# One-hot gate rows of a routed expert layer: which engine compares, which engine scales

## The chip, the cores and the metric

The kernel runs as one program on one core of one Trainium2 chip. Its time is the device time of that core in microseconds (us), from one launch to its end. Engines are named as in the profile: PE is TensorE, DVE is VectorE, ACT is ScalarE, SP issues the weight transfers.

## What is computed

The reference is a two-layer transformer block, followed by a second block of two layers whose feed-forward part is a product-key expert layer (`peer_ffn`). The change touches that last part alone, which runs twice, once for each layer:

```
idx = i1 * PEER_N_KEYS + i2            # 256 tokens x 128 choices (8 heads x 16)
g = jax.nn.softmax(best, axis=-1)
act = gelu(einsum('ckd,cd->ck', u_tab[ic], xc))
out = einsum('ck,ckd->cd', gc * act, v_tab[ic])
```

There are 128 x 128 experts, each named by a first key i1 and a second key i2. The kernel doesn't gather experts. It computes the scores of all experts and multiplies them by a dense gate matrix which is zero where a token did not choose the expert. For one token that matrix is a product of two one-hot matrices: with the token's 128 choices c as the contraction, gate[k2, k1] = sum over c of first[c, k1] * second[c, k2], where first[c, k1] is 1 where i1 of choice c is k1, and second[c, k2] is g[c] where i2 of choice c is k2, else 0.

## The kernel before

Stages follow one another: modulation, an even and an odd mixer with their feed-forward parts, then for each of two layers a mixer (class `Mixer`) and the expert layer (class `Peer`). Each engine has its own instruction list, written out in program order, and the lists meet at semaphores. Nothing is reordered at run time: an instruction that waits holds up all that stand behind it on its engine.

In `Peer`, after the queries and the early scores (`EarlyScores`: the scores of the first 33 of 128 slices of the experts), `Route` picks the experts on DVE and leaves, for all 256 tokens, the tile `slots` [128 choices, 3, 256 tokens]: gate, first key, second key. Then comes `Gates`, and after it `Experts`, which streams the u and v tables and does most of the layer's matrix work. `Experts` begins when `Gates` is done.

`Gates` takes the tokens in 64 groups of four. For each group g:

- DVE `make(g)`: one comparison of the row 0..127 (`iota`) with four tokens' second keys gives `second` [128, 4 x 128] (L1957; the tile lies in a part of `hT` that is free here, so the trace calls it hT), signal `second_made`; one with the first keys gives `first` (L1959), signal `first_made`. From g = 4 on it waits first until PE has read the buffers four groups back.
- ACT `scale(g)` waits for `second_made` and multiplies the second rows by the gates, token by token, in place: four ACTIVATEs of 128 x 128 (L1979), signal `scaled`.
- PE waits for `first_made`, for `scaled` and for its bank, and does four products of 128 x 128 x 128 into one of four PSUM banks (L1938). In the trace each product of f32 operands shows as two MATMULs, so that a group has eight.
- ACT `move_late(g)` waits for the bank and copies columns 33 to 127 of the four tokens into `gates` (L1986, 128 x 380 elements), signal `moved`.
- DVE `weigh_early(g)` waits for `moved` and multiplies the first 33 columns of the bank by the early scores (L1965, 128 x 132 elements), which frees the bank.

The order on DVE is make(g), weigh_early(g - 2), make(g + 1), and so on; on ACT it is move_late(g - 2), scale(g), move_late(g - 1), and so on. Behind the last group ACT loads the table of Gelu (`warm`, L149) and `Experts` starts with L2119 on ACT.

Of the kernel before, what the change touches and what calls it, by code (L numbers as in the profile page):

```python
# [10 lines left out]
ACT = mybir.ActivationFunctionType  # L11
ALU = mybir.AluOpType
AX = mybir.AxisListType

P = 128
# [33 lines left out]
class Span:  # L49


    def __init__(self, sem, first):
        self.sem, self.first = sem, first
# [17 lines left out]
class Use:  # L71
# [3 lines left out]
    def __init__(self, tensor, written, read):  # L75
        self.tensor, self.written, self.read = tensor, written, read
# [11 lines left out]
class Bank:  # L88
    def __init__(self, tensor, written, read):
        self.tensor, self.written, self.read = tensor, written, read  # L90
# [69 lines left out]
def hold(engine, marks):  # L160

    for sem, count in marks:
        engine.wait_ge(sem, count)
# [81 lines left out]
class Fetch:  # L245
# [7 lines left out]
    def scalar(self, after=()):  # L253
        hold(self.nc.scalar, after)
        for dst, src in self.pairs:
            self.nc.scalar.dma_start(dst, src).then_inc(self.landed.sem, 16)
# [14 lines left out]
class Modulation:  # L271
# [24 lines left out]
    def tensor(self):  # L296
        k, pe = self.k, self.k.nc.tensor
        pe.wait_ge(*self.split.after(2))
        hold(pe, self.fetch.done)
        for _ in range(4):  # L300
            pe.matmul(k.bank[7].tensor[:, 0:2], k.ones[:], k.ones[:, 0:2], start=True, stop=True)
        for b in range(self.BLOCKS + 1):
            if b == self.BLOCKS:
                self.turn(b - 1)
                break
            use = self.rows[b]
            pe.wait_ge(*use.free())
            for c in range(DC):
                hi, lo = k.ring.take()
                pe.matmul(use.tensor[0:4, :], self.parts[:, c, :], hi, start=(c == 0), stop=False)  # L310
                last = k.ring.free(pe.matmul(use.tensor[0:4, :], self.parts[:, c, :], lo, start=False,
                                             stop=(c == DC - 1)))
                if b > 0 and c == 2:
                    self.turn(b - 1)
# [497 lines left out]
class Attention:  # L812
# [6 lines left out]
    def __init__(self, k, groups, keys, span, scale, prob, turned, after):  # L819
        self.k, self.groups, self.keys, self.span, self.scale = k, groups, keys, span, scale  # L820
        self.prob, self.turned, self.after = prob, turned, after
        self.scores = [[k.bank[r].use() for r in range(4)] for _ in range(groups)]
        self.turns = [[k.bank[4 + st % 2].use() for st in range(span)] for _ in range(groups)]
        self.max = k.named("row_max").take(4 * groups)
        self.neg = k.named("row_max_negated").take(2 * groups)
        self.sunk = k.named("sink_weighed").take(2 * groups if self.sink is not None else 0)
        self.den = k.named("row_sum_inverted").take(groups)
        self.by_scalar = k.named("weights_by_scalar").take(2 * groups)
        self.by_vector = k.named("weights_by_vector").take(2 * groups)
        self.mx, self.negm, self.sums, self.rec, self.extra = (k.stats[:, :, 4 * j:4 * j + 4] for j in range(5))  # L830
# [1080 lines left out]
class Gates:  # L1911
# [5 lines left out]
    def __init__(self, k, slots, iota, early, gates, first, second, routed):  # L1917
        self.routed = routed
        self.k, self.slots, self.iota, self.early, self.gates = k, slots, iota, early, gates
        self.first, self.second = first, second  # L1920
        self.uses = [k.bank[g % 4].use() for g in range(self.GROUPS)]
        self.second_made = k.named("second_key_rows").take(self.GROUPS)
        self.first_made = k.named("first_key_rows").take(self.GROUPS)
        self.scaled = k.named("rows_scaled").take(self.GROUPS)
        self.moved = k.named("gates_moved").take(self.GROUPS)
        self.done = [u.emptied() for u in self.uses[-4:]] + [self.moved.after(self.GROUPS)]

# [3 lines left out]
    def tensor(self):  # L1931
        pe = self.k.nc.tensor
        for g, use in enumerate(self.uses):
            pe.wait_ge(*self.first_made.after(g + 1))
            pe.wait_ge(*self.scaled.after(g + 1))
            pe.wait_ge(*use.free())
            for t in range(4):
                m = pe.matmul(use.tensor[:, t * P:(t + 1) * P], self.first[:, g % 4, t, :], self.rows(g, t),  # L1938
                              start=True, stop=True)
            m.then_inc(use.written.sem, 1)  # L1940
# [7 lines left out]
                self.weigh_early(g - 2)  # L1948

    def make(self, g):  # L1950
        dve = self.k.nc.vector
        row_no = self.iota[:].unsqueeze(1).to_broadcast([P, 4, P])
        tokens = slice(4 * g, 4 * g + 4)
        keys = [self.slots[:, j, tokens].unsqueeze(2).to_broadcast([P, 4, P]) for j in (1, 2)]
        if g >= 4:
            dve.wait_ge(*self.uses[g - 4].full())
        dve.tensor_tensor(self.second[g % 4], row_no.rearrange("p (c k) n -> p c k n", c=2),  # L1957
                          keys[1].rearrange("p (c k) n -> p c k n", c=2), ALU.is_equal).then_inc(self.second_made.sem, 1)
        dve.tensor_tensor(self.first[:, g % 4], row_no, keys[0], ALU.is_equal).then_inc(self.first_made.sem, 1)  # L1959

    def weigh_early(self, g):
        dve, use = self.k.nc.vector, self.uses[g]
# [3 lines left out]
                          ALU.mult).then_inc(use.read.sem, 1)  # L1966

    def scalar(self):
        for g in range(self.GROUPS + 2):
            if g >= 2:  # L1970
                self.move_late(g - 2)
            if g < self.GROUPS:
                self.scale(g)

    def scale(self, g):
        act = self.k.nc.scalar
        act.wait_ge(*self.second_made.after(g + 1))
        for t in range(4):
            m = act.activation(self.rows(g, t), self.rows(g, t), ACT.Copy,  # L1979
                               scale=self.slots[:, 0, 4 * g + t:4 * g + t + 1])  # L1980
        m.then_inc(self.scaled.sem, 1)

    def move_late(self, g):
        act, use = self.k.nc.scalar, self.uses[g]
# [460 lines left out]
```

## Time and profile before

| | |
|---|---|
| median of 3 runs | 3836.66 us |
| fastest run | 3831.36 us |
| slowest run | 11778.27 us |
| the profiled execution: its own time | 3843.8 us |
| its span, first to last instruction | 3842.5 us |
| mean granted clock of PE over the span | 0.923 |
| PE busy | 3449.5 us (90%) |
| DVE busy | 2288.9 us (60%) |
| ACT busy | 1810.7 us (47%) |

The shares of busy time are means over all stages. What the change can do is read in the two windows in which `Gates` runs, 1868.8 to 1984.1 us (first layer) and 3081 to 3196 us (second layer) from the start of the span. The slowest run stands far from the other two; the median is one of these two.

### The profile page before, as it was taken

The page shows a single profiled execution, that of the slowest core. Times are in us where ns is not written, and L with a number is a line of the kernel's source. Part 1 is how long each engine was busy: PE and PEld are TensorE (multiplying, and loading weights), DVE is VectorE, ACT ScalarE, POOL GpSimd, SP SyncE. Part 2 cuts the span into 40 slices and gives each one's busy share as a digit, 9 for nine tenths or more (in the row PEclk, how much of TensorE's full clock was granted, in tenths as well). Part 3 has the DMA queues.
Part 4 walks back from the last instruction along what each step waited for, and adds up shares of the span by engine and source line. Part 5 has one row for each costly group of instructions (what it writes and reads, how often), then busy time and mean ns, then how long its engine had stood idle before and what let it go on. Part 6 is the DMA issues. An engine that isn't in the chain of part 4 may idle for free.

```text
span 3842.5 us, 51118 instructions
## 1 busy us (share of the span) xinstructions
PE 3449.5 (90%) x19132; PEld 2853.0 (74%) x19132; DVE 2288.9 (60%) x4729; ACT 1810.7 (47%) x3796; POOL 0.2 (0%) x4
## 2 busy tenths in 40 slices
PE   7899889999979989589779999998869968999999
PEld 2474447887748988388668999997659857899998
DVE  6633334333465645768876666665665986666665
ACT  6622333332344534252585555554334196555554
POOL 0000000000000000000000000000000000000000
PEclk9897888999889989589999999998769999999999
DMA  8820001223203543044115555553204403555554
GB/s 310 286 99 11 1 23 66 99 90 94 94 5 110 179 139 122 0 138 143 66 53 184 186 187 187 186 186 128 72 26 161 160 1 125 186 186 186 186 186 154
DMA packets 134925, 479.90 MB, mean 125 GB/s; under 512 B 15384, under 2 KB 17304, under 8 KB 133912
## 3 DMA queue, kind: packets, MB, share of 16 engines
q1 hardware_dynamic: 130352, 463.53, 36.1%
q10 hardware_dynamic: 4328, 13.11, 0.9%
q8 instruction: 154, 2.52, 0.3%
q14 instruction: 91, 0.75, 0.1%
HBM read 475.53 MB, written 1.05 MB: 124 GB/s over the span
## 4 chain that ended last, share of the span: by engine, by line
PE 83%; DVE 9%; issue 3%; DMA 3%; ACT 3%; ACTq 0%; DVEq 0%
PE bank L608 14%; PE bank L610 13%; PE bank L609 13%; PE bank L2089 6%; PE bank L2088 6%; PE bank L2090 6%; PE bank L2014 6%; PE bank L1938 4%; PE bank L475 3%; PE bank L882 3%; DMA raw<-in_mod_w 2%; DVE conv L1313 1%; PE bank L484 1%; PE bank L892 1%; PE bank L1119 1%
## 5 line engine op out<-in xcount | busy, mean ns | idle before, releaser
L223 DVE TENSOR_TENSOR w_lo<-raw,w_hi 128x512 fp32r<-128x512 f32 x1664 | 1124.5, 691 | 798.3 <-ACT w_hi L214 769.0
L214 ACT ACTIVATE w_hi<-raw 128x512 fp32r<-128x512 f32 x1664 | 1011.9, 626 | 814.3 <-PE bank L610 606.6
L608 PE MATMUL bank<-x_hi,w_hi 128*128 128x256 f32 x2096 | 597.5, 285 | 14.9 <-DVE w_lo L223 7.3
L609 PE MATMUL bank<-x_lo,w_hi 128*128 128x256 f32 x2096 | 595.5, 284 | 0.0
L610 PE MATMUL bank<-x_hi,w_lo 128*128 128x256 f32 x2096 | 593.4, 283 | 0.0
L608 PEld LDWEIGHTS bank<-x_hi,w_hi 128*128 128x128 f32 x2096 | 398.1, 190 | 26.4 <-issue 8.2
L2088 PE MATMUL bank<-w_hi,wt_hi 128*128 128x512 f32 x1024 | 406.2, 397 | 6.5 <-DVE wt_lo L2146 6.5
L2089 PE MATMUL bank<-w_lo,wt_hi 128*128 128x512 f32 x1024 | 407.5, 398 | 0.0
L2090 PE MATMUL bank<-w_hi,wt_lo 128*128 128x512 f32 x1024 | 405.8, 396 | 0.0
L609 PEld LDWEIGHTS bank<-x_lo,w_hi 128*128 128x128 f32 x2096 | 398.2, 190 | 8.0
L610 PEld LDWEIGHTS bank<-x_hi,w_lo 128*128 128x128 f32 x2096 | 399.9, 191 | 0.0
L608 PE MATMUL bank<-a_hi,w_hi 128*128 128x512 f32 (+1 forms) x880 | 309.1, 351 | 18.0 <-DVE a_lo L580 18.0
L610 PE MATMUL bank<-a_hi,w_lo 128*128 128x512 f32 (+1 forms) x880 | 303.9, 345 | 0.0
L609 PE MATMUL bank<-a_lo,w_hi 128*128 128x512 f32 (+1 forms) x880 | 302.0, 343 | 0.0
L2014 PE MATMUL bank<-xn,u_raw 128*128 128x256 f32 x1056 | 228.2, 379 | 0.0
L2088 PEld LDWEIGHTS bank<-w_hi,wt_hi 128*128 128x128 f32 x1024 | 193.5, 189 | 45.9 <-DVE wt_lo L2146 6.9
L2090 PEld LDWEIGHTS bank<-w_hi,wt_lo 128*128 128x128 f32 x1024 | 193.2, 189 | 46.2
L1938 PE MATMUL bank<-hT,first 128*128 128x128 f32 x1024 | 147.5, 289 | 83.1 <-issue 77.2
L2089 PEld LDWEIGHTS bank<-w_lo,wt_hi 128*128 128x128 f32 x1024 | 193.8, 189 | 38.0
L2014 PEld LDWEIGHTS bank<-xn,u_raw 128*128 128x128 f32 x1056 | 200.5, 190 | 27.2
L1938 PEld LDWEIGHTS bank<-hT,first 128*128 128x128 f32 x1024 | 127.0, 195 | 103.7 <-issue 97.4
L608 PEld LDWEIGHTS bank<-a_hi,w_hi 128*128 128x128 f32 x880 | 167.6, 190 | 47.3 <-issue 13.9
(318 smaller groups left out, 4947.5 us busy)
## 6 DMA issues: line engine op xcount, KB each, us to landing
raw<-in_v SPq DMA_DIRECT2D x256, 512.0 KB, 4.4
raw<-in_u SPq DMA_DIRECT2D x190, 512.0 KB, 3.5
raw<-in_mod_w SPq DMA_DIRECT2D x96, 512.0 KB, 4.8
raw<-in_w_gate_up SPq DMA_DIRECT2D x88, 512.0 KB, 3.5
u_raw<-in_u SPq DMA_DIRECT2D x66, 512.0 KB, 3.5
raw<-in_w_in SPq DMA_DIRECT2D x40, 512.0 KB, 4.0
raw<-in_w_down SPq DMA_DIRECT2D x32, 512.0 KB, 3.5
raw<-in_w_peer SPq DMA_DIRECT2D x32, 512.0 KB, 3.9
```

Of the source, the lines that this page charges most:

```text
L214: self.nc.scalar.activation(self.hi[:, m % 4, :], self.half(m), ACT.Copy).then_inc(self.rounded[m % 4], 1)
L223: self.nc.vector.tensor_tensor(self.lo[:, m % 4, :], self.half(m), self.hi[:, m % 4, :], ALU.subtract).then_inc(self.ready[m % 4], 1)
L475: m = pe.matmul(self.sums.tensor[:, 4 * at:4 * at + P // group], k.sq[:, n % 4, t * P:(t + 1) * P], indicators[group], start=(n == 0 and t ...
L608: pe.matmul(out[:, 0:width], hi[:, w], x_hi, start=(c == 0), stop=False)
L609: pe.matmul(out[:, 0:width], hi[:, w], x_lo, start=False, stop=False)
L610: mm = pe.matmul(out[:, 0:width], lo[:, w], x_hi, start=False, stop=(c == total - 1))
L882: m = pe.matmul(use.tensor[:, 0:self.keys[r]], l, x, start=(j == 0), stop=(j == len(pairs) - 1))
L1938: m = pe.matmul(use.tensor[:, t * P:(t + 1) * P], self.first[:, g % 4, t, :], self.rows(g, t), start=True, stop=True)
L2014: m = pe.matmul(use.tensor[:, 0:LAT], self.raw[:, t % 3, c * P:(c + 1) * P], self.xn[:, c, :], start=(c == 0), stop=(c == DC - 1))
L2088: pe.matmul(out, self.wt_hi[:, s, rows], hi, start=(t == 0), stop=False, skip_group_check=True)
L2089: pe.matmul(out, self.wt_hi[:, s, rows], lo, start=False, stop=False, skip_group_check=True)
L2090: m = pe.matmul(out, self.wt_lo[:, s, rows], hi, start=False, stop=(t == NKEY - 1), skip_group_check=True)
```

## The change

On DVE the comparison of the second keys and the multiplication by the gate become one `tensor_scalar` for each token, with two operands of one value per partition (second key and gate): four instructions of 128 x 128 in place of one of 128 x 512. The comparison of the first keys stays one instruction, but of three tokens (128 x 384). ACT no longer scales. It makes the first-key row of the fourth token instead, in two dependent steps: Abs(key - iota), then Relu(1 - that), which is 1 where the key is met and 0 elsewhere. Its wait for `second_made` goes; it waits once for the route's result and, from g = 4 on, for the buffers. PE waits for `first_made`, `second_made` and `last_made`.

```
-        self.scaled = k.named("rows_scaled").take(self.GROUPS)
+        self.last_made = k.named("first_key_last_row").take(self.GROUPS)
...
             pe.wait_ge(*self.first_made.after(g + 1))
-            pe.wait_ge(*self.scaled.after(g + 1))
+            pe.wait_ge(*self.second_made.after(g + 1))
+            pe.wait_ge(*self.last_made.after(g + 1))
...
     def make(self, g):
-        dve = self.k.nc.vector
-        row_no = self.iota[:].unsqueeze(1).to_broadcast([P, 4, P])
-        tokens = slice(4 * g, 4 * g + 4)
-        keys = [self.slots[:, j, tokens].unsqueeze(2).to_broadcast([P, 4, P]) for j in (1, 2)]
+
+        dve, n = self.k.nc.vector, 4 * g
         if g >= 4:
             dve.wait_ge(*self.uses[g - 4].full())
-        dve.tensor_tensor(self.second[g % 4], row_no.rearrange("p (c k) n -> p c k n", c=2),
-                          keys[1].rearrange("p (c k) n -> p c k n", c=2), ALU.is_equal).then_inc(self.second_made.sem, 1)
-        dve.tensor_tensor(self.first[:, g % 4], row_no, keys[0], ALU.is_equal).then_inc(self.first_made.sem, 1)
+        for t in range(4):
+            m = dve.tensor_scalar(self.rows(g, t), self.iota[:], self.slots[:, 2, n + t:n + t + 1],
+                                  self.slots[:, 0, n + t:n + t + 1], ALU.is_equal, ALU.mult)
+        m.then_inc(self.second_made.sem, 1)
+        dve.tensor_tensor(self.first[:, g % 4, 0:3], self.iota[:].unsqueeze(1).to_broadcast([P, 3, P]),
+                          self.slots[:, 1, n:n + 3].unsqueeze(2).to_broadcast([P, 3, P]),
+                          ALU.is_equal).then_inc(self.first_made.sem, 1)
...
     def scalar(self):
+        hold(self.k.nc.scalar, self.routed)
         for g in range(self.GROUPS + 2):
             if g >= 2:
                 self.move_late(g - 2)
             if g < self.GROUPS:
-                self.scale(g)
-
-    def scale(self, g):
-        act = self.k.nc.scalar
-        act.wait_ge(*self.second_made.after(g + 1))
-        for t in range(4):
-            m = act.activation(self.rows(g, t), self.rows(g, t), ACT.Copy,
-                               scale=self.slots[:, 0, 4 * g + t:4 * g + t + 1])
-        m.then_inc(self.scaled.sem, 1)
+                self.last_row(g)
+
+    def last_row(self, g):
+
+        k, act, row = self.k, self.k.nc.scalar, self.first[:, g % 4, 3]
+        if g >= 4:
+            act.wait_ge(*self.uses[g - 4].full())
+        away = k.sstep(act.activation(row, self.iota[:], ACT.Abs, bias=self.slots[:, 1, 4 * g + 3:4 * g + 4],
+                                      scale=-1.0))
+        act.wait_ge(*away)
+        act.activation(row, row, ACT.Relu, bias=self.k.ones[:, 0:1], scale=-1.0).then_inc(self.last_made.sem, 1)
```

## Rows read from the trace of the kernel before

**Rows 1.** Busy time of each engine in the two windows of `Gates` (x: instructions).
```profile
core 0: us, PE busy (x) PEld busy (x) DVE busy (x) ACT busy (x) POOL busy (x), PEclk, DMA share, GB/s
1869.00:1987.00 118.00, 74.24 (x514) 63.92 (x515) 105.13 (x195) 115.67 (x325) 0.00 (x0) 0.98 0.00 1
3081.00:3200.00 119.00, 75.36 (x517) 64.80 (x518) 105.46 (x195) 115.65 (x325) 0.00 (x0) 0.97 0.00 1
```

**Rows 2.** Who waited for whom in 1869 to 1987 us: total, times, longest.
```profile
PE bank L1938 <- issue: 38.6, 62, 0.6
```

**Rows 3.** Instructions in order of time, 1918 to 1922 us: start, length, engine, line.
```profile
1918.48 0.97 ACT L1986 ACTIVATE gates<-bank 128x380 f32<-128x380 f32 x1
...
1918.84 1.13 PE L1938 MATMUL bank<-hT,first 128*128 128x128 f32 x8 [0.63 <-issue]
1919.10 1.39 ACT L1979 ACTIVATE hT<-hT,slots 128x128 f32<-128x128 f32 x4
1919.49 0.43 DVE L1965 TENSOR_TENSOR early<-bank,early 128x132 f32<-128x132 f32 x1
1919.83 0.68 DVE L1957 TENSOR_TENSOR hT<-iota,slots 128x512 f32<-128x512 f32 x1
1920.24 0.97 ACT L1986 ACTIVATE gates<-bank 128x380 f32<-128x380 f32 x1
...
1920.59 1.13 PE L1938 MATMUL bank<-hT,first 128*128 128x128 f32 x8 [0.62 <-issue]
```

**Rows 4.** In order of time, the stage's first groups, 1868 to 1875 us.
```profile
1868.79 0.69 DVE L1957 TENSOR_TENSOR hT<-iota,slots 128x512 f32<-128x512 f32 x1
1869.39 0.68 DVE L1959 TENSOR_TENSOR first<-iota,slots 128x512 f32<-128x512 f32 x1
1869.51 2.48 ACT L1979 ACTIVATE hT<-hT,slots 128x128 f32<-128x128 f32 x8 [3.76 <-DVE hT L1957]
...
1870.89 3.75 PE L1938 MATMUL bank<-hT,first 128*128 128x128 f32 x16 [2.94 <-DVE first L1959]
```

**Rows 5.** In order of time, the stage's last group, 1982 to 1984 us.
```profile
1982.13 1.13 PE L1938 MATMUL bank<-hT,first 128*128 128x128 f32 x8 [0.63 <-issue]
...
1983.30 0.80 ACT L1986 ACTIVATE gates<-bank 128x380 f32<-128x380 f32 x1 [0.56 <-PE bank L1938]
```

**Rows 6.** Groups of DVE instructions over the whole span, shapes kept apart: busy, mean ns.
```profile
L970 DVE TENSOR_SCALAR prob<-prob,stats 128x512 f32<-128x512 f32 x32 | 14.7, 482 | 0.3
L458 DVE COPY spread<-mean_col 128x512 f32<-128x512 f32 x15 | 6.4, 427 | 0.5
L1872 DVE TENSOR_SCALAR part_i<-best_i 128x128 uint32<-128x128 uint32 x8 | 1.8, 223 | 0.1
L1310 DVE TENSOR_SCALAR conv<-pad,gvec 128x256 f32<-128x256 f32 x4 | 1.2, 350 | 0.1
L1869 DVE TENSOR_TENSOR res<-best 128x128 f32<-128x128 f32 x4 | 1.2, 292 | 0.1
```

**Rows 7.** DVE in order of time: two TENSOR_SCALAR in a row, at two places.
```profile
1565.78 0.62 DVE L1310 TENSOR_SCALAR conv<-pad,gvec 128x256 f32<-128x256 f32 x2
...
348.19 0.75 DVE L970 TENSOR_SCALAR prob<-prob,stats 128x256 f32<-128x256 f32 x2
```

**Rows 8.** Groups of ACT instructions over the whole span: with a value per partition, and without.
```profile
L561 ACT ACTIVATE a_hi<-a_scaled,modT 128x256 fp32r<-128x256 f32 x56 | 27.6, 506 | 24.7 <-DVE a_scaled L573 24.7
L517 ACT ACTIVATE x_hi<-xn 128x256 fp32r<-128x256 f32 x16 | 6.6, 417 | 7.8 <-DVE xn L528 7.8
```

**Rows 9.** L1979 alone in 1868 to 1878 us: least, median and greatest length.
```profile
L1979 ACT ACTIVATE hT<-hT,slots x20: 355/387/403, 1869.5 to 1877.9; 128x128 f32<-128x128 f32 x20
```

**Rows 10.** ACT in order of time: a load of a function table, and two dependent steps.
```profile
8.25 1.28 ACT L336 ACT_TABLE_LOAD   x1
9.54 0.22 ACT L336 ACTIVATE silu_c<-cT 128x16 f32<-128x16 f32 x1
9.79 0.22 ACT L338 ACTIVATE parts<-silu_c 128x16 fp32r<-128x16 f32 x1
```

## The prediction

> **What bounds the kernel now.** Read first the busy time in the two windows of `Gates`: ACT is busy for 115.67 of 118 us, DVE for 105.13, PE for 74.24, and no data moves [rows 1]. Both layers look alike, so one is worked out and doubled. Then the waits: PE has 62 short waits of 0.6 us, one for almost every group, put down to "issue" [rows 2]. The order of time says what they are [rows 3]. ACT's four scalings run from 1919.10 to 1920.49 and PE's next group starts at 1920.59, so PE starts each time 0.10 us behind the last scaling. DVE's L1965 starts at 1919.49, just behind the end of the copy L1986 (1918.48 + 0.97 = 1919.45), and so DVE too is kept by ACT. ACT itself never stops: copy to copy is 1.76 us (1918.48 to 1920.24), of which copy to first scaling is 0.62 and the four scalings 1.14, or 0.285 each. ACT bounds the stage, at 1.755 us per group, the mean over many groups (between the PE starts 1918.84 and 1920.59 it is 1.75).
>
> The stage lasts from the first comparison, 1868.79, to the end of the last copy, 1984.10: 115.3 us [rows 4, 5]. Twice that is 6% of the span, which is the ceiling of what can happen here in either direction unless the stage becomes much longer. Behind it everything is released by it: `Experts` starts when ACT has done the last copy and the table load, so each microsecond of the stage is one of the kernel. What ran before is finished and no transfer is due in it, so nothing outside covers a gain or a loss.
>
> **What ACT does after.** It loses four scalings, 1.14 us, and gets two dependent steps. Neither function is in this trace; their cost is that of ACTIVATEs of the size with a value per partition. L1979 is such a one, 355 to 403 ns long [rows 9], and 128x256 with a bias per partition is 506 against 417 ns without [rows 8], so the kind of value hardly matters. The wait between the steps costs the overlap: two dependent steps stand 0.25 apart at a length of 0.22, a gap of 0.03 [rows 10]. So: copy to Abs 0.62, Abs to Relu 0.39 + 0.03 = 0.42, Relu to the next copy 0.285, sum 1.32 us per group. The other bound is the ring through PE: move_late(g) stands before last_row(g + 2), and PE(g) between last_row(g) and move_late(g). From rows 3 to 5: 0.10 to start PE, 1.13 of PE, 0.04 to start the copy, 0.62 + 0.42 + 0.39 until the Relu's end, in all 2.70 us for two groups, 1.35 for one. ACT and this ring therefore allow 1.32 to 1.35 and are left 0.4 below the time of now. The new hold for the route is met when DVE begins; ACT sits idle there anyhow (3.76 us) [rows 4].
>
> **What DVE does after.** This decides. Now it needs, when nothing holds it, 0.60 for each comparison of 128x512 (1868.79 to 1869.39) [rows 4] and 0.34 for L1965 (1919.49 to 1919.83) [rows 3]: 1.54 per group. After:
> - The comparison of three tokens: TENSOR_TENSORs of 128x512 and of 128x128 last 0.685 us [rows 4] and 0.292 us (L1869) [rows 6], so a column costs 1.02 ns. 128 columns fewer make 0.60 - 0.13 = 0.47.
> - Four TENSOR_SCALARs of 128x128. Columns: with one value per partition 128x512 takes 482 ns and 128x256 350 ns [rows 6], so 256 columns cost 132 ns, half of what a TENSOR_TENSOR takes for them, and 128 cost 66. Fixed: two of 128x256 in a row cover 0.62 at 0.35 each, so they start 0.27 apart [rows 7]; less 0.13 for columns that leaves nearly 0.14, and 0.20 for each of 128x128, if the second value per partition costs nothing more.
> - The price of a value per partition: 482 ns against 427 for a COPY of the same size with none (L458) [rows 6], 55 ns. No row has two. The second is worth between 0 (fetched beside the first) and 55 ns (fetched after it), so 0.20 to 0.255 each, four of them 0.79 to 1.02.
> - An upper bound for the fixed part: the two L970 of 128x256 start 0.75 - 0.35 = 0.40 apart [rows 7]. If that is the rule for the kind of instruction, it leaves up to 0.27 fixed and 0.33 each. They work in place, which the new ones don't; L1310 reads one tile and writes another as the new ones do, so it is the nearest row.
> - L1965 is unchanged, 0.34 to 0.35.
>
> With the second value free: 0.79 + 0.47 + 0.35 = 1.61 us per group. With it at full price: 1.02 + 0.47 + 0.35 = 1.84. Both lie over ACT's 1.35: DVE takes ACT's place as the bound, and the question is on which side of 1.755 it comes out. There is no row that tells the two apart. I take the first: the 55 ns are a latency rather than a quantity (one value in each partition), and latencies of two reads of one instruction need not add up. That is an argument and no measurement, so both ends stay in the range.
>
> A rule speaks against my fixed part. The Trainium skill, "VectorE: DVE Perf Modes", section on the TRN2 errata, gives VectorE SBUF to SBUF 58 cycles and the columns over the mode's factor, 120 from PSUM. By it the new list would be 4 x 0.127 + 0.46 + 0.26 = 1.23 us, less than ACT's bound (an estimate from that page). The page itself says that this row comes out too short for one instruction alone. The trace's 0.14 fixed for one with a value per partition is more than double its 0.06, and L1965's 0.34 is over its 0.26.
>
> **PE.** It has one wait more. Its group takes 1.13 [rows 3], under 1.61, so it isn't the bound. Its start is now released by DVE's last comparison instead of ACT's scalings. The granted clock in the window is 0.98 now [rows 1]; a busier PE gives no ground for a lower one, and I take it as it is.
>
> **The sum.** DVE's list from the first TENSOR_SCALAR to the end of the last comparison: 64 x (0.79 + 0.47) = 80.6 and 62 x 0.35 = 21.7, 102.3 us. Behind it 0.08 for the end of that comparison, 0.10, PE 1.13, 0.04 and the copy 0.80 [rows 5]: 2.15. At the start PE's first two groups go at half pace (3.75 for 16 MATMULs against 1.13 for 8) [rows 4] and make DVE's first waits for a copy come late by about 0.5. Stage: 105.0 us against 115.3, 10.3 less, twice 20.6. The profiled execution would go from 3843.8 (span 3842.5 and 1.3 around it) to 3823.2. It lies 7.1 over the median of the runs; from 3836.66 the forecast is 3816 us, 0.54% less.
>
> **The rivals.**
> - Second value at full price (slower than before). The list is 64 x (1.02 + 0.47) + 21.7 + 2.15 = 119.2 us, 3.9 more than now, twice 7.8: 3844 us. DVE is the place, the fetch of the gate the price; it decides from 0.235 us per TENSOR_SCALAR on, where 4 x 0.235 + 0.82 meets 1.755. For it: one value costs a visible 55 ns. Against it: nothing but the argument above.
> - A dearer TENSOR_SCALAR: a spacing of 0.33 as the in-place pairs show, or a fused comparison that is given only a TENSOR_TENSOR's pace, one column per 1.02 ns. At 0.33, 4 x 0.13 = 0.52 more per group, 67 us over the forecast: 3883. At the slow pace, 4 x 0.065 x 128 = 33 more: 3849, or 3877 with the second value dear as well. Against it: L1872, an integer shift of 128x128, takes 223 ns [rows 6], 69 less than the TENSOR_TENSOR of 128x128, so it has the quick pace.
> - Cheap DVE, ACT's ring the bound: 64 x 1.35 + 3 = 89 us per stage, 26 less, twice 52: 3784. It needs TENSOR_SCALARs 0.13 apart, and no row is so quick. The errata row of the page named above would give this.
> - Abs and Relu not in the loaded table. Each load takes 1.28 [rows 10]; with two per group ACT would need 1.32 + 2.57 = 3.89, the stage 252 us, the kernel 4110. Against it: Copy, Square and Identity run between Exp, Sqrt and Gelu here with no load of their own. The Trainium skill, "ScalarE: Activation LUTs", section on table sets, says that relu, copy, identity and abs are in every set; no run here shows it of Abs and Relu.
> - The change does nothing that can be seen: DVE's spacing happens to be 0.22 to 0.24, the stage stays at 1.7 to 1.76 and ACT's relief is idle time. This is the middle of the first two cases: 3825 to 3837.
>
> **How the numbers follow.** Forecast case (second value free or nearly) 0.45; at full price 0.33; the middle 0.07; dearer TENSOR_SCALAR 0.08; cheap DVE 0.05; table loads 0.02. The forecast's own range is 3808 to 3824, from 0.19 to 0.21 per TENSOR_SCALAR and the edges of the stage. The range over cases has to hold forecast, middle and full price (0.85), whose ends with some microseconds of spread between runs (the two close ones are 5 us apart) are 3806 and 3856. A change within 2% (77 us, about what a measurement of this kernel can tell from no change) covers all but table loads and a very dear TENSOR_SCALAR: 0.03 slower, 0.01 faster.
>
> **What would show it.** In the changed profile: DVE busy without gaps through the stage and ACT with an idle time of some 0.3 us per group; the group's period (from one L1965 to the next) 1.61 if right, 1.84 if the second value costs; the TENSOR_SCALAR's length 0.28 against 0.34; its starts 0.20 or 0.255 apart; PE's gaps of 0.6 shrunk to 0.48 and ended by DVE; the Abs to Relu distance 0.42; one ACT_TABLE_LOAD at the stage's end and none inside. What would make me wrong beyond the cases: a wait of DVE at L1965 for the copy in each group, which would mean that the ring through PE is longer than the 1.35 worked out.

## The result and the profile after

The changed kernel takes 3843.09 us (median of 15 runs) against 3835.70 us (the kernel before, 15 runs too); ratio 1.0016, 95% interval 1.0009 to 1.0023. It is slower by some 6 us, which is little, but the interval excludes 1. Ratios here and below compare fast runs alone, without one run of 11778.27 us of the kernel before and one of 8801.40 us of the kernel with three rows scaled and one fused. The forecast was 3816 us; the rival with the second value at full price had 3844. Which of the two it is stands in the stage itself.

Busy time of each engine in the two windows of the stage, changed kernel (answers to [rows 1]):

```profile
core 0: us, PE busy (x) PEld busy (x) DVE busy (x) ACT busy (x) POOL busy (x), PEclk, DMA share, GB/s
1869.00:1987.00 118.00, 75.37 (x498) 62.60 (x496) 111.25 (x363) 87.00 (x188) 0.00 (x0) 0.97 0.02 5
3081.00:3200.00 119.00, 76.00 (x508) 63.35 (x508) 113.92 (x373) 89.34 (x194) 0.00 (x0) 0.97 0.01 4
```

In this execution the stage begins and ends some microseconds earlier than in the one of before, so that the windows also hold some 8 us of `Experts` in the first layer. The exchange is plain all the same: ACT falls from 115.67 to 87.00 us, DVE rises from 105.13 to 111.25. A window that lies inside the first layer's stage in both executions shows it clean, first before, then after (columns as above):

```profile
1880.00:1960.00 80.00, 51.55 (x366) 44.31 (x367) 74.12 (x138) 80.00 (x230) 0.00 (x0) 1.00 0.00 1
```
```profile
1880.00:1960.00 80.00, 50.96 (x352) 42.59 (x352) 80.00 (x264) 60.82 (x132) 0.00 (x0) 1.00 0.00 1
```

Before, ACT was the engine that never stopped; after, DVE is. The waits of the first layer's stage (answers to [rows 2]) name the new bound:

```profile
PE bank L1939 <- DVE first L1960: 39.4, 60, 0.7
ACT gates L1992 <- PE bank L1939: 24.3, 59, 1.0
DVE early L1968 <- ACT gates L1992: 1.4, 1, 1.4
```

PE waits in each group for DVE's last comparison, ACT waits in each group for PE, and DVE waits once, for the last copy, when all its comparisons are done. One group in order of time (answers to [rows 3]):

```profile
1918.62 0.41 DVE L1968 TENSOR_TENSOR early<-bank,early 128x132 f32<-128x132 f32 x1
...
1918.75 0.36 ACT L1984 ACTIVATE first<-iota,slots 128x128 f32<-128x128 f32 x1
1918.75 1.16 PE L1939 MATMUL bank<-hT,first 128*128 128x128 f32 x8 [0.66 <-DVE first L1960]
1918.95 1.10 DVE L1957 TENSOR_SCALAR hT<-iota,slots 128x128 f32<-128x128 f32 x4
1919.14 0.40 ACT L1987 ACTIVATE first<-first,ones 128x128 f32<-128x128 f32 x1
1919.95 0.82 ACT L1992 ACTIVATE gates<-bank 128x380 f32<-128x380 f32 x1 [0.40 <-PE bank L1939]
1919.97 0.54 DVE L1960 TENSOR_TENSOR first<-iota,slots 128x384 f32<-128x384 f32 x1
1920.44 0.41 DVE L1968 TENSOR_TENSOR early<-bank,early 128x132 f32<-128x132 f32 x1
```

Read the starts on DVE, not the lengths: product to first TENSOR_SCALAR 0.33, four TENSOR_SCALARs 1.02, comparison to product 0.47, in all 1.82 us from product to product. 1.02 for four is 0.255 each. Over the whole run:

```profile
L1957 DVE TENSOR_SCALAR hT<-iota,slots x512: 327/331/468, 1861.1 to 3191.5; 128x128 f32<-128x128 f32 x171
L1984 ACT ACTIVATE first<-iota,slots x128: 357/366/401, 1861.1 to 3190.6; 128x128 f32<-128x128 f32 x128
L1960 DVE TENSOR_TENSOR first<-iota,slots x128: 537/541/676, 1862.2 to 3191.7; 128x384 f32<-128x384 f32 x128
```

A TENSOR_SCALAR with two values per partition lasts 0.331 us, where 0.28 had been expected with one price and 0.34 with two. The stage's edges, first steps and table load of each layer:

```profile
1861.13 1.11 DVE L1957 TENSOR_SCALAR hT<-iota,slots 128x128 f32<-128x128 f32 x4
...
1979.08 1.28 ACT L149 ACT_TABLE_LOAD   x1
...
3194.48 1.28 ACT L149 ACT_TABLE_LOAD   x1
```

From first step to table load the stage takes 117.95 us, and 115.3 before ([rows 4, 5]; the last copy's end is 1984.10). The second layer's stage, 3076.54 to 3194.48, takes 117.9, and 115.3 before. That is 2.6 us more in each, 5.3 in all, inside the interval of the ratio (3 to 9 us). There is no load of a table inside the stage. Nothing outside it is needed to explain the result. The two profiled executions as wholes can't show it: they took 3843.8 us before and 3843.66 after, because the rest of the kernel differs by as much from run to run as the stages do by the change.

### The profile page after: what moved, and what is told of

Same layout as the page of the kernel before. It is cut to its first block, busy times and chain, and to the rows that moved or that the text cites. A ratio compares the mean times of both kernels' runs of the same rounds, so it can differ in the third digit from the quotient of the medians.

```text
span 3842.3 us, 51376 instructions
## 1 busy us (share of the span) xinstructions
PE 3446.5 (90%) x19132; PEld 2850.7 (74%) x19132; DVE 2314.0 (60%) x5113; ACT 1762.4 (46%) x3540; POOL 0.2 (0%) x4
## 4 chain that ended last, share of the span: by engine, by line
PE 78%; DVE 15%; DMA 3%; ACT 3%; issue 1%; ACTq 0%; DVEq 0%
PE bank L608 14%; PE bank L610 13%; PE bank L609 13%; PE bank L2095 6%; PE bank L2094 6%; PE bank L2096 6%; PE bank L2020 6%; DVE hT L1957 3%; PE bank L475 3%; DMA raw<-in_mod_w 3%; PE bank L882 2%; DVE first L1960 2%; DVE conv L1313 1%; DVE early L1968 1%; PE bank L484 1%
```

## The experiments

The nine kernels below were each timed beside runs of the kernel before, four runs for most, ten for "changed without the last row" and "three scaled, one fused", six for "GpSimd fuses one". "Stage" is the first layer's, from DVE's first step to the table load, in the profiled execution; "group" is the spacing of DVE's products or of ACT's copies in the steady part.

| kernel | group, us | stage, us | ratio to before | 95% interval |
|---|---|---|---|---|
| before | 1.755 | 115.3 | 1 | |
| changed | 1.82 | 117.9 | 1.0016 | 1.0009 to 1.0023 |
| one value, two operations | 1.58 | 103.2 | 0.9942 | 0.9925 to 0.9958 |
| one value, one operation | 1.58 | 103.1 | 0.9938 | 0.9921 to 0.9954 |
| no value, two operations | 1.43 | 94.9 | 0.9898 | 0.9882 to 0.9915 |
| all first rows on DVE | 1.95 | 127.0 | 1.0060 | 1.0044 to 1.0077 |
| changed without the last row | 1.82 | 117.9 | 1.0018 | 1.0005 to 1.0030 |
| before with three scalings | 1.53 | 101.0 | 0.9930 | 0.9904 to 0.9957 |
| three scaled, one fused | 1.65 | 107.9 | 0.9972 | 0.9958 to 0.9987 |
| GpSimd scales one | 1.54 | 102.3 | 0.9931 | 0.9909 to 0.9953 |
| GpSimd fuses one | 1.46 | 97.6 | 0.9920 | 0.9901 to 0.9939 |

**What makes a TENSOR_SCALAR dear.** Theory 1: the values per partition are fetched one after the other. Theory 2: the second arithmetic operation costs time. Theory 3: this kind of instruction has a floor at 0.257 us. Three kernels differ in the per-token step alone.

```
# changed
m = dve.tensor_scalar(self.rows(g, t), self.iota[:], self.slots[:, 2, n + t:n + t + 1],
                      self.slots[:, 0, n + t:n + t + 1], ALU.is_equal, ALU.mult)
# one_value_two_ops
m = dve.tensor_scalar(self.rows(g, t), self.iota[:], self.slots[:, 2, n + t:n + t + 1], 1.0, ALU.is_equal, ALU.mult)
# one_value_one_op
m = dve.tensor_scalar(self.rows(g, t), self.iota[:], self.slots[:, 2, n + t:n + t + 1], None, ALU.is_equal)
# no_value_two_ops
m = dve.tensor_scalar(self.rows(g, t), self.iota[:], 5.0, 0.01, ALU.is_equal, ALU.mult)
```

> The changed kernel, but the per-token comparison multiplies by the constant 1.0 and not by the token's gate (left out: the gates' weight). Theory 1, values per partition are fetched one after the other at 0.055 us each: the four TENSOR_SCALARs start 0.20 us apart where the changed kernel has 0.257, the group takes 0.80 + 0.79 = 1.59 us against 1.82, and the kernel is 24 us faster than before (ratio 0.994). Theory 2, the second arithmetic operation costs it: still 0.257 apart, 1.82 us per group, 6 us slower than before (ratio 1.0016). Theory 3, nothing starts closer than 0.257 for this kind of instruction: as theory 2.

> The changed kernel, but the per-token step only compares (one value per partition, one operation; left out: the gates' weight). Theory 1: as with two operations, 0.20 us apart, 1.59 us per group, 24 us faster than before (0.994). Theory 2: 0.20 apart here and 0.257 with two operations. Theory 3: 0.257 apart, ratio 1.0016.

> The changed kernel, but the per-token step compares with the constant 5 and multiplies by the constant 0.01 (left out: second keys and gates). Theory 1: no value to fetch, 0.145 us apart, DVE's list 0.58 + 0.79 = 1.37 us per group, just over the 1.35 worked out for the ring through PE and ACT; 50 us faster than before (0.987). If the ring is really longer, the group takes the ring's time and DVE shows a wait for the copy in each group. Theory 2: 0.257 apart and 1.82 us. Theory 3: the same.

The step's instructions over the whole run (least, median and greatest length), in the order of the three kernels:

```profile
L1957 DVE TENSOR_SCALAR hT<-iota,slots x512: 267/280/356, 1863.1 to 3165.2; 128x128 f32<-128x128 f32 x171
```
```profile
L1957 DVE TENSOR_SCALAR hT<-iota,slots x512: 267/279/333, 1860.2 to 3162.1; 128x128 f32<-128x128 f32 x171
```
```profile
L1957 DVE TENSOR_SCALAR hT<-iota x512: 206/220/234, 1864.9 to 3151.2; 128x128 f32<-128x128 f32 x171
```

Median lengths of 0.331, 0.280 and 0.220 us for two values, one and none; the least lengths, 0.327, 0.267 and 0.206, stand 0.06 apart at both steps. One operation or two is the same, 0.279 and 0.280. The starts say it too. Four in a row, in order of time, one kernel after the other (one value and two operations; one value and one; none and two):

```profile
1920.24 0.90 DVE L1957 TENSOR_SCALAR hT<-iota,slots 128x128 f32<-128x128 f32 x4
...
1921.02 0.58 DVE L1960 TENSOR_TENSOR first<-iota,slots 128x384 f32<-128x384 f32 x1
```
```profile
1920.48 0.86 DVE L1957 TENSOR_SCALAR hT<-iota,slots 128x128 f32<-128x128 f32 x4
...
1921.26 0.54 DVE L1960 TENSOR_TENSOR first<-iota,slots 128x384 f32<-128x384 f32 x1
```
```profile
1921.46 0.61 DVE L1957 TENSOR_SCALAR hT<-iota 128x128 f32<-128x128 f32 x4
...
1922.00 0.54 DVE L1959 TENSOR_TENSOR first<-iota,slots 128x384 f32<-128x384 f32 x1
```

First step to the comparison behind it is 1.02 us with two values, 0.78 with one and 0.54 with none: 0.255, 0.195 and 0.135 each, steps of 0.06. Theories 2 and 3 fall, and of theory 1 the price stands: each value adds 0.06, also the second. That the values are fetched one after the other is the picture behind it, which no run shows. The ratios are 0.9942 and 0.9938; theory 1 expected 0.994 for both kernels, theory 2 only for the one with one operation, theory 3 for neither (1.0016).

The price is the same with far fewer columns, as two groups of the kernel before show, whose instructions have two. L935 has no value per partition, L959 has one (`lam`), and both have one operation:

```profile
L935 DVE TENSOR_SCALAR stats<-stats 128x2 f32<-128x2 f32 x56 | 9.5, 169 | 1.9
L959 DVE TENSOR_SCALAR stats<-stats,lam 128x2 f32<-128x2 f32 x8 | 1.8, 228 | 0.3
```

That is 0.059 us for one value at two columns, against 0.06 at 128.

In the third kernel theory 1's gain of 50 us was missed; the gain is 39 us (1 - 0.9898 of 3836). DVE's list of 1.34 no longer bounds it: from its comparison to its product it now takes 0.54 us in the median, against 0.47 where nothing holds it. The ring through ACT and PE bounds it, and it is longer than worked out:

```profile
1920.23 0.82 ACT L1991 ACTIVATE gates<-bank 128x380 f32<-128x380 f32 x1
...
1920.58 1.13 PE L1939 MATMUL bank<-hT,first 128*128 128x128 f32 x8 [0.42 <-ACT first L1986]
...
1920.85 0.36 ACT L1983 ACTIVATE first<-iota,slots 128x128 f32<-128x128 f32 x1
...
1921.24 0.40 ACT L1986 ACTIVATE first<-first,ones 128x128 f32<-128x128 f32 x1
...
1921.74 0.85 ACT L1991 ACTIVATE gates<-bank 128x380 f32<-128x380 f32 x1
1921.90 1.13 PE L1939 MATMUL bank<-hT,first 128*128 128x128 f32 x8 [0.19 <-ACT first L1986]
```

The Relu ends at 1921.64 and PE starts at 1921.90, 0.26 later (0.25 in the median of the steady part); behind the scalings of before it was 0.10 [rows 3]. With 0.26 in the place of 0.10 the ring is 2.86 us for two groups, 1.43 for one, and 1.43 is the mean spacing of the copies. Why PE starts later here is open. It need not be the Relu: where GpSimd's row is the last to come (in "GpSimd scales one", below), PE also starts 0.25 behind it, and both signals are the third that PE's list waits for, while the scalings' is the second and that of DVE's first-key comparison, behind which PE starts after 0.05, the first. Engine, function and place in the list were not taken apart.

**Whether ACT has a part in the 1.82 us.** Two kernels: one takes the last row from ACT and gives it to DVE; the other takes it from ACT and gives it to nobody.

```
# all_first_rows_on_vector: last_row(g) and PE's wait for it go
-        dve.tensor_tensor(self.first[:, g % 4, 0:3], self.iota[:].unsqueeze(1).to_broadcast([P, 3, P]),
-                          self.slots[:, 1, n:n + 3].unsqueeze(2).to_broadcast([P, 3, P]),
+        dve.tensor_tensor(self.first[:, g % 4], self.iota[:].unsqueeze(1).to_broadcast([P, 4, P]),
+                          self.slots[:, 1, n:n + 4].unsqueeze(2).to_broadcast([P, 4, P]),
# changed_without_last_row: last_row(g) and PE's wait for it go
-                m = pe.matmul(use.tensor[:, t * P:(t + 1) * P], self.first[:, g % 4, t, :], self.rows(g, t),
+                m = pe.matmul(use.tensor[:, t * P:(t + 1) * P], self.first[:, g % 4, min(t, 2), :], self.rows(g, t),
```

> The changed kernel with all four first-key rows made by DVE and none by ACT; nothing left out. If DVE's list alone bounds the stage, each group takes 128 columns more, 1.82 + 0.13 = 1.95 us, 17 us over the changed kernel and 23 us over before (ratio 1.006). If ACT's two dependent steps have a part in the 1.82 us, taking them away gives some of it back: under 1.95 us per group and a ratio under 1.004.

> The changed kernel without ACT's two steps (PE uses the third token's first-key row for the fourth too, so the fourth token's gates are wrong). If DVE's list alone sets the 1.82 us, taking 0.8 us of ACT's work away changes nothing: 1.82 us per group, ratio 1.0016 to before as the changed kernel has. If the two dependent steps on ACT have a part in it, it gets faster than the changed kernel.

Measured: 1.0060, where 1.006 stood for DVE's list alone and under 1.004 for a part of ACT, and 1.0018 without the row, where 1.0016 was expected. In the latter ACT is busy for only 35.78 us of 80 (columns as in the first fence of the result):

```profile
1880.00:1960.00 80.00, 50.97 (x352) 42.59 (x352) 80.00 (x265) 35.78 (x45) 0.00 (x0) 1.00 0.00 1
```

DVE has no gap, and the stage lasts 117.9 us with or without ACT's row. ACT and its two dependent steps are off the path. They are worth what they take from DVE: 0.13 us per group, the 17 us between the ratios 1.0060 and 1.0016. In the kernel with all first rows on DVE the granted clock of PE is 0.87 in the mean over the 80 us from 1880 us, so that it is at the lower of its two levels for part of them, where it is 1.00 in the changed kernel; PE idles 0.80 us in front of a group there, against 0.66. This has no part in the ratio: DVE's starts keep their spacing of 0.256, 0.60 and 0.33 us, and PE still waits for DVE.

**What relieving ACT is worth by itself, and better shares.** First the kernel before with one scaling left out:

```
-        for t in range(4):
+        for t in range(3):
             m = act.activation(self.rows(g, t), self.rows(g, t), ACT.Copy,
```

> The kernel before with one of ACT's four scalings left out (the fourth token's gates are missing). If ACT's list bounds the kernel before, ACT falls to 1.48 us per group and DVE's two wide comparisons and its product, 0.60 + 0.60 + 0.34 = 1.54, take over: 26 us faster (0.993), which is what relieving ACT alone is worth. If ACT was not the bound, no change.

Measured 0.9930, a group of 1.53 us, and DVE full but for the stage's last waits (78.65 of the 80 us from 1880 us, and the stage ends at 1960.4). ACT did bound the kernel before, and one scaling less is enough to lift it off; DVE's two wide comparisons then hold the stage. So the change took far more from ACT than could be used, and paid for it on the engine that came next.

The second kernel splits the rows otherwise. DVE compares the second keys of three tokens and fuses the fourth; it makes all first-key rows; ACT scales three rows:

```
dve.tensor_tensor(self.second[:, g % 4, 0:3], ... self.slots[:, 2, n:n + 3] ..., ALU.is_equal)   # 128x384
dve.tensor_scalar(self.rows(g, 3), self.iota[:], self.slots[:, 2, n + 3:n + 4], self.slots[:, 0, n + 3:n + 4],
                  ALU.is_equal, ALU.mult)
dve.tensor_tensor(self.first[g % 4], ..., ALU.is_equal)                                          # 128x512
```

> A mixture that computes everything: DVE compares the second keys of three tokens (128x384) and makes the fourth token's row in the fused step, and all four first-key rows; ACT scales three rows and makes none. (The two row tiles change places, so that three rows of second keys lie side by side.) By the costs measured so far: DVE 0.47 + 0.257 + 0.60 + 0.34 = 1.67 us per group, ACT 0.62 + 3 x 0.285 = 1.48, so DVE bounds at 1.67 against 1.755 before and 1.82 in the changed kernel: 11 us faster than before, ratio 0.997. If a fused step costs more when it stands between two comparisons, or the work doesn't divide like this, no gain.

Measured 0.9972, with DVE busy for the whole of an 80 us window and a group of 1.65 us. A single fused step pays; four don't, since each adds 0.255 us to DVE and takes away only 0.13.

The last two use GpSimd, which does nothing in either kernel. In one it scales the fourth row in place of ACT, in the other it makes the fourth token's fused row in place of DVE:

```
# pool_scales_one: kernel before, ACT scales three
gp.wait_ge(*self.second_made.after(g + 1))
gp.tensor_scalar(self.rows(g, 3), self.rows(g, 3), self.slots[:, 0, 4 * g + 3:4 * g + 4], None, ALU.mult)
# pool_fuses_one: as three_scaled_one_fused, but on GpSimd
gp.tensor_scalar(self.rows(g, 3), self.iota[:], self.slots[:, 2, 4 * g + 3:4 * g + 4],
                 self.slots[:, 0, 4 * g + 3:4 * g + 4], ALU.is_equal, ALU.mult)
```

> The kernel before, computing everything, with GpSimd scaling the fourth row in place of ACT (ACT scales three). If GpSimd takes under 1.5 us for 128x128 and disturbs nobody: ACT 1.48, DVE 1.54 us per group, so 1.55, 26 us faster than before (0.993). If GpSimd and DVE hinder each other when both read the row buffers, DVE's comparisons get longer than 0.685 us and the gain is lost; if GpSimd's step takes 2 us or more, it bounds the stage and the kernel is 30 us or more slower (1.008).

Measured 0.9931. Its rows, lengths over the whole run:

```profile
L1959 DVE TENSOR_TENSOR hT<-iota,slots x128: 671/682/708, 1854.6 to 3154.7; 128x512 f32<-128x512 f32 x128
L1989 POOL TENSOR_SCALAR hT<-hT,slots x128: 795/980/1498, 1855.4 to 3155.5; 128x128 f32<-128x128 f32 x128
```

GpSimd takes 0.98 us for the row, where a DVE step with one value is 0.28 us long. PE waits for this row in nearly every group (44 times between 1880 and 1950 us), but PE isn't the bound, so the length is hidden: the group's 1.54 us are DVE's list. DVE's comparisons keep their starts 0.602 us apart beside it, as before. GpSimd is the one that changes: its row is 0.795 us long at the least, in the third group, while DVE mostly stands still, and 1.3 to 1.5 in the first two groups, where DVE compares without a pause. So the two do seem to hinder each other, and here it costs nothing; no run takes this apart.

> The mixture with three scaled rows, but the fourth token's fused row is made by GpSimd and not by DVE; everything is computed. DVE keeps 128x384, 128x512 and its product: 0.47 + 0.60 + 0.34 = 1.41 us per group; ACT 0.62 + 3 x 0.285 = 1.48; GpSimd took 0.98 us for a 128x128 step with one value per partition, and with two it should stay under 1.4. Then ACT bounds at 1.48: 35 us faster than before (ratio 0.991), 9 us faster than with GpSimd scaling. If the second value costs GpSimd much more (over 0.5 us), it bounds instead, and the ratio is 0.993 or worse.

Measured: 3806.71 us against 3835.14, 0.9920 where 0.991 was expected, the fastest of those that compute everything. Its interval overlaps that of the kernel where GpSimd scales, so which of the two is faster is open in the times; the groups are 1.46 against 1.54 us. GpSimd's step has a median of 1.475 us here:

```profile
L1970 POOL TENSOR_SCALAR first<-iota,slots x128: 789/1475/2062, 1869.4 to 3154.8; 128x128 f32<-128x128 f32 x128
```

That is not the price of the second value. The step's least length is 0.789 us, as it was with one value (0.795), and three such steps follow each other 0.78 us apart early in the stage, from 1873.15 us, while DVE mostly stands still:

```profile
L1970 POOL TENSOR_SCALAR first<-iota,slots x3: 789/790/791, 1873.2 to 1874.7; 128x128 f32<-128x128 f32 x3
```

Later in the stage three engines are busy for 80 of 80 us:

```profile
1880.00:1960.00 80.00, 61.94 (x440) 53.23 (x440) 80.00 (x165) 80.00 (x220) 80.00 (x55) 1.00 0.01 1
```

Which of them holds the stage can be read from the order of time:

```profile
1919.26 0.90 ACT L1999 ACTIVATE gates<-bank 128x380 f32<-128x380 f32 x1
...
1919.53 1.13 PE L1940 MATMUL bank<-first,hT 128*128 128x128 f32 x8 [0.33 <-issue]
1919.87 1.02 ACT L1992 ACTIVATE first<-first,slots 128x128 f32<-128x128 f32 x3
...
1920.71 0.90 ACT L1999 ACTIVATE gates<-bank 128x380 f32<-128x380 f32 x1
...
1920.99 1.13 PE L1940 MATMUL bank<-first,hT 128*128 128x128 f32 x8 [0.33 <-issue]
```

ACT does. Its scalings end at 1920.89 and PE starts at 1920.99, 0.10 behind them as in the kernel before. ACT never stops, and its starts are as close as they were there: 0.61 from the copy to the first scaling and 0.85 for three, 1.46 in all (1.48 had been worked out). GpSimd has its row of a group ready 3.0 us before the last scaling of that group, and this lead is the same from the eighth group to the last, so PE never waits for it. DVE's list is 1.41; its full 80 us are lengths that stretch over a short wait.

## Why the prediction was wrong

**The step that failed** is the price of the second value per partition, which the part on DVE put at nothing: "I take the first: the 55 ns are a latency rather than a quantity (one value in each partition), and latencies of two reads of one instruction need not add up." The runs show that the costs do add up: 0.135, 0.195 and 0.255 us from start to start for none, one and two. Four TENSOR_SCALARs cost 1.02 and not 0.79 us per group. That is the whole miss: 0.23 us x 128 groups is 29 us, of which the product's spacing, 0.33 and not 0.35, gives 2.5 back, and 3816 + 29 - 2.5 is 3842.6, with 3843.1 measured. In the stage the miss is 117.95 against 105.0 us. The range held the time; the forecast was on the wrong side of no change, with 0.33 given to the case that came true against 0.45.

What the rows had to say was the price of one value, 55 ns, and 60 is what it measured. With a visible price for one, "each costs as much" was the plain reading; setting it at nothing needed an argument from outside the rows. The trace of before even had that price a second time, in a TENSOR_SCALAR itself: 59 ns between L935 and L959. The two-operation part of the instruction, which had been given no price, has none.

**What held.** ACT bound the kernel before (0.9930 with one scaling less, as expected). DVE takes over as the bound. A comparison of 128x384 to the next step: 0.47 worked out, 0.47 measured. The product L1968 to the next step: 0.34 to 0.35 worked out, 0.33 measured. A TENSOR_SCALAR with one value: 0.20 against 0.195. With one value the stage was forecast at 105.0 us and the kernel with one value shows 103.2. The full-price rival had a group of 1.84 us, a stage of 119.2 and 3844 us; measured are 1.82, 117.9 and 3843.1. It was 1.3 us per stage too long because the product's spacing is 0.33 and not 0.35. That it comes within 1 us of the measured time is partly luck: its change was 7.8 us, the stages show 5.3 and the ratio says 3 to 9.

**What was off without weight.** ACT's list: Abs to Relu 0.40 us against 0.42. The ring through PE and ACT: 1.43 against 1.35, for PE's start 0.25 and not 0.10 us behind the Relu; it stays under DVE's 1.82, so it had no part in this result, and cost some 10 us in the kernel with no values. The 0.5 us at the stage's start: DVE's first product comes 0.15 us late.

**The other rivals.** A dearer TENSOR_SCALAR from the in-place pairs of 128x256 (0.33 apart, 3883 us) did not come, so the spacing of those pairs has another cause, which was not looked into. Cheap DVE (3784 us) fell: the steps start 0.255 us apart, and only without a value do they come near 0.13, at 0.135. The Trainium skill, "VectorE: DVE Perf Modes", section on the TRN2 errata, puts such a step at 0.127 us (an estimate from its 58 cycles and half the columns at 0.96 GHz). The trace agrees for the step without values, 0.135, and not for the one with two, 0.255; so the reservation about that row was right for this kernel, but for the values and not for the row itself. Table loads (4110 us) did not come: the trace has no load between the stage's first step and its end, with Copy, Abs and Relu taking turns. The Trainium skill, "ScalarE: Activation LUTs", section on table sets, says that these three are in every set, and the trace agrees.

## What to carry to other kernels

Fusing two operations into one instruction saves the second pass over the columns, but each operand with one value per partition costs 0.06 us on DVE (0.059 at 2 columns, 0.06 at 128); at 128 columns the two values cost nearly as much, 0.12 us, as all else in the instruction, 0.135. Before moving work between engines, write both lists per group and their sums: here ACT stood at 1.755 and DVE at 1.54, so ACT needed relief of one scaling and DVE had 0.2 us to give, while the change gave ACT 0.4 and charged DVE 0.28. Where both lists are nearly full, look for a third engine that is idle: a step over three times as long on GpSimd gained 0.7 to 0.8%, because no engine that held the stage waited for it.

## What the runs showed of the hardware

- Values per partition add up on DVE: 0.220, 0.280 and 0.331 us long for none, one and two with 128x128 f32; from start to start it is 0.135, 0.195 and 0.255. A second arithmetic operation costs nothing (0.279 and 0.280).
- The length of an instruction in the trace is not what it costs its own engine. In the changed kernel's second layer L1957 reaches 0.468 us against 0.327 at the least, and the group is still 1.82 us; in the kernel before ACT's L1979 goes from 0.355 to 0.797 us while copy to copy stays at 1.755. Only the starts of neighbouring instructions give that cost. The length still counts for whoever waits for the result: in the kernel before PE starts 0.10 us behind the end of the last scaling, whether that lasted 0.39 or 0.73 us.
- PE begins 0.05 us behind DVE's first-key comparison, 0.10 behind ACT's last scaling, and 0.25 behind ACT's Relu or GpSimd's row, each where it is the last to come. The cause is open.
- GpSimd's TENSOR_SCALAR of 128x128 is 0.79 us long at the least, both with one value and one operation and with two and two; beside a busy DVE the medians are 0.98 and 1.475 us.
